# Projecting the 24 gate columns with the tokens as stationary operand, in a two-layer hybrid decoder trunk

## The reference, cut to what matters

```python
h = rms_norm(x, norm_mix)
proj = jnp.einsum('btd,dp->btp', h, w_in).astype(jnp.float32)
(g_qkv, g_z, g_b, g_a, r_q, r_k, r_v, r_g,
 m_qk, m_v, m_o, m_i, m_f) = jnp.split(proj, ...)
...
beta = jax.nn.sigmoid(b_logit).transpose(0, 2, 1)
g = (-jnp.exp(a_log) * jax.nn.softplus(a_logit + dt_bias)).transpose(0, 2, 1)
...
log_i = (i_logit + i_bias).transpose(0, 2, 1)
log_f = jax.nn.log_sigmoid(f_logit + f_bias).transpose(0, 2, 1)
```

## Time and profile before

| | |
|---|---|
| median of 3 runs | 1043.15 us |
| lowest and highest run | 1042.1 and 1043.86 us |
| span of the profiled execution, first to last instruction | 1041.0 us |
| TensorE busy, weight loads busy | 871.2 us, 629.5 us |
| VectorE, ScalarE, GpSimd busy | 353.5 us, 219.6 us, 28.2 us |
| mean granted clock of TensorE | 0.945 of full speed |

### The profile page before, as it was taken

How to read it: one execution, slowest core, us unless ns; L and a number is a source line. 1 busy time by engine, 2 the same in 40 slices (tenths; PEclk the granted TensorE clock), 3 DMA queues, 4 the chain that set the end, 5 groups by cost and what they waited for, 6 DMA issues and landing times.

```text
span 1041.0 us, 18150 instructions
## 1 busy us (share of the span) xinstructions
PE 871.2 (84%) x6932; PEld 629.5 (60%) x6933; DVE 353.5 (34%) x787; ACT 219.6 (21%) x416; POOL 28.2 (3%) x28
## 2 busy tenths in 40 slices
PE   5999999989588767798679999999895887879765
PEld 3877887978364434444358778879784543445332
DVE  1656634424621011111126565344346111112102
ACT  1233322322311010011103342133113111111111
POOL 2000000000300000000000000000003000000000
PEclk9999999999989898899879999999998998989888
DMA  9913012434459999989955120134334799899992
GB/s 343 353 47 102 1 41 82 162 122 162 168 229 419 420 420 421 421 326 421 401 190 182 40 82 1 42 122 162 113 150 168 302 421 421 339 423 419 420 421 109
DMA packets 48480, 249.47 MB, mean 240 GB/s; under 512 B 6096, under 2 KB 18560, under 8 KB 19344
## 3 DMA queue, kind: packets, MB, share of 16 engines
q1 hardware_dynamic: 47824, 246.91, 59.8%
q0 software_dynamic: 576, 1.43, 0.5%
HBM read 247.50 MB, written 1.05 MB: 239 GB/s over the span
## 4 chain that ended last, share of the span: by engine, by line
PE 49%; DMA 23%; DVE 13%; issue 7%; PEld 3%; ACT 2%; PEldq 1%; SPq 1%; DVEq 1%; POOLq 0%; ACTq 0%
DMA ring<-e_down 18%; PE ps L480 15%; PE ps L940 5%; PE ps L782 5%; PE ps L910 4%; PE ps L495 3%; PE ps L879 3%; DMA shared<-e_down 3%; DVE kq L1432 3%; DMA ring<-e_up 2%; DVE shared L1437 2%; PEld ps L910 1%; PE ps L679 1%; PE ps L634 1%; PE ps L951 1%
## 5 line engine op out<-in xcount | busy, mean ns | idle before, releaser
L480 PE MATMUL ps<-hT,ring 128*128 128x256 f32 x864 | 190.8, 380 | 0.0
L480 PEld LDWEIGHTS ps<-hT,ring 128*128 128x128 f32 x864 | 162.9, 190 | 25.4 <-DVEq L1249 2.0
L910 PE MATMUL ps<-ring,hT 128*32 128x256 f32 x1728 | 115.3, 426 | 42.8 <-DMA ring<-e_up 21.4
L910 PEld LDWEIGHTS ps<-ring,hT 128*32 128x32 f32 x1728 | 66.9, 122 | 91.1 <-issue 70.2
L879 PEld LDWEIGHTS ps<-kq 128*128 128x128 bf16 x960 | 64.9, 149 | 10.0 <-issue 7.4
L951 PE MATMUL ps<-hT,kq 128*128 128x512 f32 x144 | 66.1, 602 | 5.6 <-PE ps L940 5.6
L879 PE MATMUL ps<-kq 128*128 128x128 bf16 x960 | 67.7, 234 | 2.3 <-DVE kq L1617 2.3
L940 PE MATMUL ps<-ring,kq 128*32 128x512 f32 x448 | 52.6, 610 | 14.1 <-DMA ring<-e_down 10.1
L1617 DVE TENSOR_TENSOR kq<-shapes,sel 128x128 bf16<-128x128 f32 (+1 forms) x40 | 9.9, 288 | 158.1 <-PE ps L918 157.8
L782 PE MATMUL ps<-ring,xn 128*128 128x256 f32 x256 | 57.8, 381 | 0.0
L910 PE MATMUL ps<-shared,hT 128*32 128x256 f32 x576 | 40.0, 439 | 20.2 <-DMA shared<-e_up 18.7
(11 more groups left out here) (305 smaller groups left out, 1029.1 us busy)
## 6 DMA issues: line engine op xcount, KB each, us to landing
ring<-e_gate SPq DMA_DIRECT2D x48, 1024.0 KB, 21.7
ring<-e_up SPq DMA_DIRECT2D x48, 1024.0 KB, 11.0
ring<-e_down SPq DMA_DIRECT2D x48, 1024.0 KB, 23.7
ring<-w_mix SPq DMA_DIRECT2D x34, 1024.0 KB, 10.1
shared<-e_down SPq DMA_DIRECT2D x16, 1024.0 KB, 7.8
shared<-e_gate SPq DMA_DIRECT2D x16, 1024.0 KB, 18.8
shared<-e_up SPq DMA_DIRECT2D x16, 1024.0 KB, 26.5
ring<-w_mix SPq DMA_DIRECT2D x12, 512.0 KB, 7.1
```

What stands on the lines that cost most here:

```text
L480: mm = pe.matmul(bank[:, ct * T:(ct + 1) * T], w[:, k, ct * P:(ct + 1) * P], hT3[:, k, :], start=(k == 0), stop=(k == KD - 1))
L910: mm = pe.matmul(ps[32 * e:32 * e + 32, 5 + m, 0:DE], hq[:, k, 32 * e:32 * e + 32], slot[at[e]][:, k * DE:(k + 1) * DE], start=(k == 0), s ...
```

## The change

The gate columns are multiplied with the roles of the operands exchanged: a tile of `hT` (128 model columns x 128 tokens) is the stationary operand and the 24 weight columns are moving, for each of the two token tiles and the eight k tiles. The result stands in PSUM with tokens on partitions, at columns 0 and 128 of the bank, where the transposes put it before. The copy to `lgT` and the two transposes are gone, and with them the name `gatesT`; `gates` takes its place in the list of banks, which has 134 names now. `project_cm` of slot 1 joins the loop over the other four. The two later waits on `lgT_ready` count one less.

```diff
--- before.py
+++ after.py
@@ -67,7 +67,7 @@
 C_I = C_MO + MW
 D_IN = C_I + 2 * MH
 NG = 2 * GH + 2 * MH
-PROJ = [("gatesT", [(C_B, 2 * GH), (C_I, 2 * MH)])]
+PROJ = [("gates", [(C_B, 2 * GH), (C_I, 2 * MH)])]
 PROJ += [(("gdn", s), [(COLS * s, min(COLS, 3 * GW - COLS * s))]) for s in range(5)]
 PROJ += [(("gate", 0), [(C_Z, COLS)]), (("gate", 1), [(C_Z + COLS, P)]), (("gate", 2), [(C_RG, RW)]),
          (("gate", 3), [(C_MO, COLS)]), (("gate", 4), [(C_MO + COLS, P)])]
@@ -103,7 +103,7 @@
 
 def psum_plan():
 
-    order = [("hT", i) for i in range(4)] + ["gatesT", ("gdn", 0), "gates"] + [("gdn", s) for s in range(1, 5)]
+    order = [("hT", i) for i in range(4)] + ["gates", ("gdn", 0)] + [("gdn", s) for s in range(1, 5)]
     order += ["rows", "cols", ("gate", 0), ("beta", 0), ("beta", 1)] + [("nrm", s) for s in range(3)] + [("gate", 1)]
     order += [("vt", p) for p in range(GP)] + [("dec", 0)]
     for h in range(GH):
@@ -419,7 +419,7 @@
                 pool.sem_inc(first, 1)
                 pool.dma_start(par_next[:, :], params[l + 1]).then_inc(par_in, 16)
 
-                pool.wait_ge(lgT_ready, 2)
+                pool.wait_ge(lgT_ready, 1)
                 for j in range(TT):
                     pool.wait_ge(part_ready, j + 1)
                     pool.tensor_tensor(rest[:, j, :], xn3[:, j, :], part[0][:, j, :], ALU.subtract).then_inc(rest_ready, 1)
@@ -520,19 +520,15 @@
                 pe.wait_ge(init_done, 6)
                 pe.wait_ge(hT_ready, 4)
 
-                bank = begin("gatesT")
+                bank = begin("gates")
                 have_slot(lap, 0)
-                for k in range(KD):
-                    mm = pe.matmul(bank[0:NG, 0:T], slot_w(0)[:, k, 0:NG], hT3[:, k, :], start=(k == 0), stop=(k == KD - 1))
-                done(mm, "gatesT")
-                held.append("gatesT")
-                project_cm(("gdn", 0), lap)
-                bank = begin("gates")
-                pe.wait_ge(lgT_ready, 1)
                 for j in range(TT):
-                    mm = pe.transpose(bank[:, j * P:(j + 1) * P], lgT[:, j * P:(j + 1) * P], c("ident"))
+                    for k in range(KD):
+                        mm = pe.matmul(bank[:, j * P:j * P + NG], hT3[:, k, j * P:(j + 1) * P], slot_w(0)[:, k, 0:NG],
+                                       start=(k == 0), stop=(k == KD - 1))
                 done(mm, "gates")
-                for s in range(1, 5):
+                held.append("gates")
+                for s in range(5):
                     project_cm(("gdn", s), lap)
 
 
@@ -843,7 +839,7 @@
                 pe.wait_ge(full[b_], n_ + 1)
                 pe.sem_inc(logits_read, 1)
                 bank = begin("logits")
-                pe.wait_ge(lgT_ready, 2)
+                pe.wait_ge(lgT_ready, 1)
                 for j in range(TT):
                     mm = pe.transpose(bank[:, j * P:(j + 1) * P], lgT[:, j * P:(j + 1) * P], c("ident"))
                 done(mm, "logits")
@@ -1292,10 +1288,6 @@
                 dve.wait_ge(init_done, 6)
                 link(dve.memset(cin_g[:, :, 0:3], 0.0))
 
-                bank = get("gatesT")
-                link(dve.tensor_copy(lgT[0:NG, :], bank[0:NG, 0:T]))
-                dve.sem_inc(lgT_ready, 1)
-                free_("gatesT")
                 bank = get("gates")
                 b3 = bank[:, 0:TT * P].rearrange("p (j c) -> p j c", j=TT)[:, :, 0:NG]
                 bias = pv("bias3", 0, 24).unsqueeze(1).to_broadcast([P, TT, 24])
```

## The result

The changed kernel takes 1046.84 us (median of 8 runs, 1043.86 to 1048.04), the kernel before 1043.34 us in the same comparison (8 runs, 1038.99 to 1044.06). The ratio is 1.0035, with a 95% interval of 1.0020 to 1.0049: slower by 3.5 us, where 1040.8 us was forecast. Rival 1, the starved clock, had been given 1047.4 us. One of the 27 runs of the kernel before that stand beside `e5` to `e8` took 2779.62 us and is in no ratio.

What follows compares the result with a forecast made beforehand. TensorE, busy 84% of the span, was taken as the bound. Transposes and bank plan, (0.21 + 0.95) x 2 = 2.3 us off the 1041.0 us span, gave 1038.7, adjusted by 2.15 to 1040.8 us; range 1039.6 to 1048.0.

Steps and rivals of the forecast that it cites:

- Rival 1: Projection starves TensorE's clock into conv slot 0; 6.5 us lost in both layers, 1047.4 us; chance 0.32, one layer 0.09.
- The projection: Gate columns ahead of conv slot 0: 32 records of 0.111 us, 3.55 us against 3.55 now; taken as 0.
- The two transposes: Between conv slots 0 and 1 on TensorE: their removal gains 0.21 us per layer.
- The copy and the earlier gate arithmetic: DVE's 0.41 us copy and 6.84 us wait disappear, gate arithmetic runs beside conv slot 0; valued at nothing.
- Rival 3: DVE's or ACT's head start reaches past the convolutions: up to 2.5 us a layer, 1036 us; chance 0.03.
- The bank plan: m_out(0)'s bank follows em 1 instead of ms 3, so it starts earlier: 0.95 us gained per layer.
- Rival 2: m_out(0) waits for something unseen beside ms 3, so only 0.4 us is left: 1042.7 us; chance 0.09.
- The clock: Layer 2's projection starts at 1.2 GHz; with the clock returning as before, it ends at 536.0 us as before.
- If the clock returns at the same time: Layer 2's projection: 3.3 us at half pace, then 17 records of 0.111 us; forecast with clock unharmed, chance 0.47.
- The row called a warning: L510's transposes, half loads and half streaming, kept TensorE busy 3.68 of 4.1 us at 0.50 without lifting the clock.

Runs made afterwards that it cites:

- e5: Changed kernel with the matmuls of the new projection and of conv slot 0 taken in turns; 1044.23 us, 1.002 of the kernel before.
- e8: Changed kernel with 120 moving columns in the projection and the bank plan of before; 1042.04 us, 0.9999 of the kernel before.
- e1_wide: Changed kernel with the 24 weight columns moved five times over (120 moving columns); 1039.43 us, 0.9969 of the kernel before.
- e3_behind: Changed kernel with the new projection placed behind conv slot 0 instead of ahead of it; 1040.27 us, 0.9977 of the kernel before.
- the square: Ratios to before: 24 moving columns, 1.0035 (again 1.0033) with changed banks, 1.0049 with old; 120 columns, 0.9969 and, bottom right, 0.9999.
- e2_banks: Kernel before with banks 4 and 5 exchanged, so m_out(0)'s tile follows em 1; 1039.91 us, 0.9968 of the kernel before.
- after: The changed kernel itself, in its first profile, against the kernel before; 1046.84 us, 1.0035.
- e10_dve: Changed kernel with 120 moving columns plus an unread DVE copy where the old copy to lgT stood; 1041.43 us, one run.
- e7_after: The changed kernel once more, unaltered, against the kernel before; 1045.71 us, 1.0033.
- e4_oldbanks: Changed kernel with the bank plan of before, so only the projection differs from the kernel before; 1048.37 us, 1.0049 of it.

## Why the prediction was wrong, step by step

**The projection.** 32 x 0.111 us = 3.55 us is what the hardware does at full clock: 3.57 us in both layers of `e1_wide` and of `e8_wide_old`, 3.68 us behind a dense slot in `e3_behind`. The count and the price were right; the clock at which they apply was not. At the low clock a record took 0.212 us (6.77 us for 32), where the working had 0.222.

**The two transposes.** Right: 0.2 us per layer (34.55 us against 34.74).

**The copy and the earlier gate arithmetic.** Valued at nothing, and the bottom right corner of the square bears it out for the sum: 0.9999, in which the transposes' gain of 0.4 us and the 0.7 us of the DVE pause below are held too. There the first bias addition is at 20.22 us in layer 1, 7.2 us earlier than before, and the kernel is no faster for it. In the changed kernel's own profile it is at 23.47 us, earlier than the 27.37 us of before by less than forecast, and ScalarE takes conv slot 0 out later than before (31.90 against 29.73 us), after 5.97 us of waiting for a late TensorE. Rival 3, up to 2.5 us a layer, is out.

**The bank plan.** The step held in place and size: `m_out(0)` starts 0.11 us behind the end of the first L1135, with 0.79 us of idle in place of 1.77; counted from `rows`, `e2_banks` gains 0.93 and 0.95 us where 0.95 was taken. Rival 2, the wait that moves, is out: nothing unseen stood beside `ms 3`. Alone, in `e2_banks`, it came out faster by 0.32%, more than its 1.9 us explain.

**The clock.** This is the step that failed. The prediction went on with "If the clock returns at the same time", which its own rows left open, and gave that case 0.47 and the starved clock in both layers 0.32. The starved clock is what happens. Its rival said further that "in layer 1 the clock is high when the projection starts", from one profile; in the first profile of the changed kernel it wasn't, in the second it was, and the change lost either way. The rival's mechanism was right and its sizes nearly so: it had layer 2's low clock end at about 541 us, 10.2 us after the projection's start at 530.8, and in the two profiles it ends 10.0 and 10.5 us after it (535.1 to 545.1, 533.2 to 543.7); in place of 3.25 us per layer the square has 2.6 to 3.4 us. Its reckoning of 6.5 - 2.3 = 4.2 us of loss stands beside the measured 3.5 and 3.4 (1.0033 of 1041.95 us).

The prediction's argument against the rival was that the loads keep the array's input busy. The runs contradict it: TensorE had no gap in any of the six narrow projections ahead of slot 0, the only edit between `after` and `e1_wide` is how many columns stream behind each load, and with 24 columns the clock stayed low or fell, while with 120 it stayed high or rose. In the nine layers in which conv slot 0 began at the low clock, the clock rose inside that slot, and in layer 2 of the kernel before inside L526, which also moves 256 columns per record but has 24 of 128 weight columns in use. The row called a warning, L510 at 0.50 through 3.68 us of work, was the wrong witness: in five layers of the wide kernels the clock rose during the same transposes. The Trainium skill ("TensorE: Matmul & The Clock Gate", Part 1) has the clock throttled unless matmul activity releases it. The runs agree in so far as every rise at a layer's head came during TensorE's work or within about a microsecond behind it. In the four narrow projections that began low, 6.8 us of work without a gap did not bring it.

Between these two forms the runs settle nothing: 72 columns held the clock once and lost it once, and in `e5_mixed` it was low for 7.4 and 11.2 us though most of the time went to dense records.

**Also not foreseen.** DVE has a pause of 0.60 in place of 0.24 us before one of its products in the middle of each layer; the profile names only DVE's own previous instruction. The kernel before and the changed one, timelines of DVE:

```profile
138.85 0.69 DVE L1437 TENSOR_TENSOR shared<-shared,ps 128x512 f32<-128x512 f32 x1 [0.24 <-DVE kq L1432]
```

```profile
143.74 0.69 DVE L1429 TENSOR_TENSOR shared<-shared,ps 128x512 f32<-128x512 f32 x1 [0.60 <-DVE kq L1424]
```

It costs 0.36 us per layer and is there in all profiles with the new projection, `e8_wide_old` with the old banks and `e10_dve` with the copy among them, and not in `e2_banks`. Its cause stays open.

## What to carry to other kernels

When a matmul's operands are exchanged so that few columns move over a full weight tile, ask not only what a load costs but what the stretch does to the clock: several microseconds of such loads at the head of a stage cost this kernel twice, in the stretch and in the dense work behind it. Behind a dense slot, or with the same 24 columns moved five times over, the loss was gone (0.9977 and 0.9969). And read what an edit does by the way: here the only gain came from one name less in a list of PSUM banks, and a hand-made swap of two banks in the kernel before gives it whole, 0.9968, without the new projection.

## What the runs showed of the hardware

- A TensorE that is busy without a gap can drop from 2.4 to 1.2 GHz: at 18.1 us (`e7_after`) and at 539.2 us (`e4_oldbanks`), inside 24-column projections, and it came back inside the dense slot behind them, at 24.9 and 546.1 us. Behind a dense slot (`e3_behind`) it stayed high through the same projection in both layers.
- The clock at the start of a stage varied between profiled executions of one kernel: layer 1's projection of the changed kernel took 6.77 us in one and 5.25 us in another.
- The granted clock is printed as 1.00 before its first record, also where the pace of the loads, 0.21 us, shows 1.2 GHz.
- Three runs of the kernel before spread by 1.8 us, 26 by 4.4 us (1040.64 to 1045.08), so three runs a side could not have shown a step of 2 us.
